# Attention heads in pairs: the values of two heads in turn, one pair late

## What is computed

```python
for l in range(2):                                  # first block
    a, g, zc, q, k, v, za, qi, ki, wi = split(h @ w_in[l])
    y_conv = silu(layer_norm(depthwise_conv31(a * sigmoid(g)))) * silu(zc)
    score  = sum_heads(relu(qi @ ki.T) * wi)        # picks the 132 keys of each query
    p      = softmax(where(chosen & causal, rope(q) @ rope(k).T / 8, -inf))   # 8 heads of 64
    y_attn = (p @ v) * silu(za)
    h      = layer_norm(alpha * h + concat(y_conv, y_attn) @ w_out[l])
# second block: 8 query heads of 64 over 2 key heads, no mask, 512 x 512
p    = softmax(axial_rope(rms(q)) @ axial_rope(rms(k)).T / 8)
y_a  = ((p @ v) * silu(gate_a)) @ w_proj_attn
g    = sigmoid(g_merge + b_merge)                   # 2 x 1024 channels
y    = g[0] * y_a + g[1] * y_b                      # y_b: a gated MLP branch
out  = rmsnorm(h + y @ w_out)
```

## Time and profile before

| | us |
|---|---|
| median of 3 runs | 1139.7 (1139.41 to 1143.92) |
| the profiled execution, its own time | 1140.32 |
| its span, first to last instruction | 1138.5 |
| TensorE busy | 1069.5 (94% of the span) |
| VectorE busy | 696.3 (61%) |
| ScalarE busy | 579.9 (51%) |
| GpSimd busy | 129.7 (11%) |
| mean granted TensorE clock | 0.972 of full |

### The profile page before, as it was taken

One profiled execution on the slowest core, in us unless ns is written; L12 is line 12 of the kernel. 1 busy time (PEld: TensorE's weight loads), 2 busy tenths in 40 slices (PEclk: granted clock), 3 DMA queues, 4 the chain that ended last, 5 costly groups with the idle time before them and its releaser, 6 DMA issues.

```text
span 1138.5 us, 16658 instructions
## 1 busy us (share of the span) xinstructions
PE 1069.5 (94%) x6484; PEld 900.7 (79%) x6484; DVE 696.3 (61%) x1553; ACT 579.9 (51%) x938; POOL 129.7 (11%) x185
## 2 busy tenths in 40 slices
PE   7998999889999899889999899969999999999997
PEld 7987898857767799789888567858888777778885
DVE  3999999965554569999989554634631332232422
ACT  6574871637333548478255643444565464554331
POOL 0000100002110100010011211223200000000001
PEclk9998999989989999999999899979999999999999
DMA  8785773735101768458546520484777525344761
GB/s 283 174 186 166 163 170 96 171 63 127 49 1 37 185 134 214 118 113 196 136 115 146 112 86 1 148 199 134 176 176 207 144 75 129 94 104 119 168 165 74
DMA packets 23822, 152.36 MB, mean 134 GB/s; under 512 B 2865, under 2 KB 3377, under 8 KB 6849
## 3 DMA queue, kind: packets, MB, share of 16 engines
q0 software_dynamic: 9648, 68.75, 32.6%
q1 hardware_dynamic: 14096, 82.55, 19.8%
HBM read 149.20 MB, written 2.10 MB: 133 GB/s over the span
## 4 chain that ended last, share of the span: by engine, by line
PE 81%; ACT 7%; DMA 5%; DVE 4%; issue 2%; POOL 0%; POOLq 0%; SPq 0%; DVEq 0%; ACTq 0%
PE psum_B L1163 19%; PE psum_A L1163 13%; PE psum_B L1196 9%; PE psum_A L1196 8%; PE psum_A L1313 6%; PE psum_B L1271 3%; DMA w_lo<-in_weights 3%; PE psum_C L1219 3%; PE psum_B L1504 3%; PE psum_B L1313 2%; PE psum_A L1517 2%; DMA w_raw<-in_weights 2%; DVE conv_acc L1600 2%; PE psum_B L1517 2%; ACT w_hi L605 2%
## 5 line engine op out<-in xcount | busy, mean ns | idle before, releaser
L1600 DVE SCALAR_TENSOR_TENSOR conv_acc<-u,vec,conv_acc 128x528 f32<-128x528 f32 (+1 forms) x240 | 172.9, 756 | 3.2
L1163 PE MATMUL psum_B<-x_hi,w_hi 128*128 128x264 f32 (+3 forms) x512 | 145.4, 323 | 8.2 <-ACT shifted L660 5.6
L1163 PE MATMUL psum_B<-x_lo,w_hi 128*128 128x264 f32 (+3 forms) x512 | 143.1, 318 | 0.0
L1163 PE MATMUL psum_B<-x_hi,w_lo 128*128 128x264 f32 (+3 forms) x512 | 142.8, 317 | 0.0
L998 POOL DMA_DIRECT2D w_lo<-in_weights x67 | 60.9, 909 | 685.8 <-ACT w_lo L606 685.8
L605 ACT ACTIVATE w_hi<-w_raw 128x2048 fp32r<-128x2048 f32 (+2 forms) x87 | 129.9, 1493 | 14.8 <-DMA w_raw<-in_weights 14.5
L606 ACT ACTIVATE w_lo<-w_raw 128x2048 fp32r<-128x2048 f32 (+2 forms) x87 | 129.3, 1486 | 0.0
L1163 PE MATMUL psum_A<-x_hi,w_hi 128*128 128x264 f32 (+2 forms) x496 | 117.9, 295 | 7.2 <-DMA w_lo<-in_weights 3.3
L1163 PE MATMUL psum_A<-x_lo,w_hi 128*128 128x264 f32 (+2 forms) x496 | 115.4, 290 | 0.0
L1163 PE MATMUL psum_A<-x_hi,w_lo 128*128 128x264 f32 (+2 forms) x496 | 115.3, 290 | 0.0
L1163 PEld LDWEIGHTS psum_B<-x_hi,w_hi 128*128 128x128 f32 (+1 forms) x512 | 89.3, 190 | 19.2 <-issue 12.5
(11 more groups left out here) (323 smaller groups left out, 2234.7 us busy)
## 6 DMA issues: line engine op xcount, KB each, us to landing
w_raw<-in_weights SPq DMA_DIRECT2D x67, 1024.0 KB, 5.7
w_lo<-in_weights POOLq DMA_DIRECT2D x65, 1024.0 KB, 8.8
x_first<-in_x_t SPq DMA_DIRECT2D x4, 528.0 KB, 7.0
h<-in_x SPq DMA_DIRECT2D x1, 2048.0 KB, 9.7
out<-h SPq DMA_DIRECT2D x4, 512.0 KB, 2.6
post_ln_g<-in_post_ln_g SPq DMA_DIRECT2D x2, 512.0 KB, 3.9
post_ln_b<-in_post_ln_b SPq DMA_DIRECT2D x2, 512.0 KB, 5.6
w_raw<-in_weights SPq DMA_DIRECT2D x2, 288.0 KB, 5.4
```

What stands on the lines that cost most here:

```text
L1163: mm = pe.matmul(ps[0:cols, i, 0:b - a], w[wp][:, kt, at:at + cols], x[xp][:, kt, a:b], start=(kt == 0 and wp + xp == 0), stop=(kt == KD - ...
L1600: got = dve.scalar_tensor_tensor(dst, src, w, dst, ALU.mult, ALU.add)
```

## The change

The attention loops of both blocks go by pairs of heads.

- `probs_times_v` and `probs_times_v2` do two heads in one call, for each key tile first the even head's matmul, then the odd head's, which write to the two halves of the partitions.
- In the first block a pair's values are computed one pair late. Turned probabilities have four buffers instead of two; the two new ones lie where the convolution's input of finished channels lay. Logits are computed four items ahead (two pairs), not two. VectorE masks and normalises the pair `i + 2` before the other work of the pair `i`; ScalarE takes the exponentials of both heads of that pair after the first copy of the pair `i`.
- In the second block both transposes of a pair come before the gate product, the values of the pair after it, and then the MLP's transpose. The weight splits woven in there go one half per pair.
- `gain` and `square_early` move to other addresses, and the load of `gain` waits for the last convolution rows of layer 1. The first output product over the last tile's convolution half moves from item 38 to 39 in layer 0.

```diff
@@ probs_times_v
-                pe.wait_ge(act_took.sem, act_took.at((l, "PT", t, hd)))
-                mm = pe.matmul(out, v[0:META, 0, hd * HD:hd * HD + HD], src[0:META, t * P:t * P + n],
-                               start=True, stop=(t == 0))
-                for j in range(1, t + 1):
-                    mm = pe.matmul(out, v[:, j, hd * HD:hd * HD + HD], src[:, (j - 1) * P:(j - 1) * P + n],
-                                   start=False, stop=(j == t))
+                pe.wait_ge(act_took.sem, act_took.at((l, "PT", t, hd + 1)))
+                for j in [0] + list(range(1, t + 1)):
+                    for odd in range(2):
+                        s, col = HD * odd, (hd + odd) * HD
+                        src = pt[i % 4 + odd]
...
+                        mm = pe.matmul(ps[s:s + HD, 0, hd // 2 * P:hd // 2 * P + n], keys, probs,
+                                       start=(j == 0), stop=(j == t))
@@ TensorE, first block
+                attention_logits(l, 0)
+                attention_logits(l, 2)
+                for i in range(0, n, 2):
                     turn_probs(l, i)
                     if i:
-                        probs_times_v(l, i - 1)
-                probs_times_v(l, n - 1)
+                        probs_times_v(l, i - 2)
+                    woven(i)
+                    turn_probs(l, i + 1)
+                    if i + 4 < n:
+                        attention_logits(l, i + 4)
+                    woven(i + 1)
+                probs_times_v(l, n - 2)
@@ ScalarE, first block
+                exps(l, 0)
+                exps(l, 1)
+                for i in range(0, n, 2):
+                    take_probs_t(l, i)
+                    if i + 2 < n:
+                        exps(l, i + 2)
+                        exps(l, i + 3)
+                    woven(i)
+                    take_probs_t(l, i + 1)
+                    woven(i + 1)
@@ VectorE, first block
+                for i in range(0, n, 2):
+                    if i + 2 < n:
+                        masked_logits(l, i + 2)
+                        masked_logits(l, i + 3)
+                        normalise(l, i + 2)
+                        normalise(l, i + 3)
+                    for op in middle[i] + middle[i + 1]:
+                        y_part(l, *op[1:])
+                    woven(i)
+                    woven(i + 1)
@@ TensorE, second block
+            merge_gate(0)
+            for i in range(0, n, 2):
+                turn_probs2(i)
+                turn_probs2(i + 1)
+                if i:
                     merge_gate(i // 2)
-                if i % 2 and i < 8:
+                if i + 4 < n:
+                    logits2(i + 4)
+                    logits2(i + 5)
+                probs_times_v2(i)
+                if i < 8:
                     turn_mlp(i // 2)
```

More of the change, by code:

```diff
@@ L832, in _, with woven @@
                 n = len(items[l])
[L833 to L837, removed]
+                def woven(i):
                     for op in todo[i]:
@@ L1408, in _, with woven @@
                     pe.wait_ge(rope_made.sem, rope_made.at((l, "k", c)))
-                attention_logits(l, 0)
-                for i in range(n):
-                    if i % 2 == 0 and i + 2 < n:
-                        attention_logits(l, i + 2)
+                def woven(i):
                     for op in todo[i]:
@@ L1846, in _, with woven @@
                 n = len(items[l])
-                masked_logits(l, 0)
-                masked_logits(l, 1)
-                for i in range(n):
-                    normalise(l, i)
-                    for op in middle[i]:
-                        y_part(l, *op[1:])
-                    if i + 2 < n:
-                        masked_logits(l, i + 2)
+                def woven(i):
                     for op in todo[i]:
@@ L1871, in _ @@
                             y_part(l, *op[1:])
+                masked_logits(l, 0)
+                masked_logits(l, 1)
+                normalise(l, 0)
+                normalise(l, 1)
+                for i in range(0, n, 2):
+                    if i + 2 < n:
+                        masked_logits(l, i + 2)
[6 more added lines that the diff above has]
+                    woven(i + 1)
                 y_part(l, "attn", 4)
@@ L2089, in _ @@
             n = len(items2)
-            max2(0)
-            max2(1)
-            for i in range(n):
-                normalise2(i)
-                if i > 1 and i % HEADS == 1:
-                    attn2_part(i // HEADS - 1)
-                if i + 2 < n:
-                    max2(i + 2)
-                if i % 2 and i < 8:
+            for i in range(4):
+                max2(i)
+            normalise2(0)
+            normalise2(1)
+            for i in range(0, n, 2):
+                if i + 2 < n:
+                    normalise2(i + 2)
+                    normalise2(i + 3)
+                if i and i % HEADS == 0:
+                    attn2_part(i // HEADS - 1)
+                    attn2_lo(i // HEADS - 1)
+                if i + 4 < n:
+                    max2(i + 4)
+                    max2(i + 5)
+                if i < 8:
                     mlp_low(i // 2)
-                if i > 2 and i % HEADS == 2:
-                    attn2_lo(i // HEADS - 1)
             attn2_part(3)
```

75 lines of the change are left out of this document (38 added, 37 removed).

## The result

The changed kernel takes 1113.3 us (median of 4 runs, 1111.81 to 1114.4) against 1139.56; the ratio is 0.976, with a 95% interval of 0.9734 to 0.9786. It is faster, and inside the range given (1088 to 1129), but 15 us above the 1098 forecast. The range is 41 us wide and holds two of the three rivals too (1113 and 1128), so that being inside it decides nothing between them; the trace has to. The profiled execution took 1111.81, its span is 1110.0.

A forecast was written before the change was run, and what follows sets the result against it. TensorE, busy 1069.5 of 1138.5 us, was taken as the bound, with VectorE nearer from 197 to 249. Gains 15.5 + 3.6 + 15.4 + 4 + 8 - 2 - 2 = 42.5 off 1140.3 gave 1098 us, range 1088 to 1129.

The forecast's parts named there:

- Halves overlap: Value matmuls: two heads on different column halves take one head's time, 16 passes in 1.02 us; chance .72, forecast 1098.
- Layer 0 from 249: First block, layer 0, from 249 us: 15.4 us saved on 14 pairs' values, plus 4 us of waits recovered.
- the dip at 331 us: Layer 0, 331.6 to 341 us: granted clock .69 behind the longest wait for probabilities, 2.9 us lost.
- my 6.8: Layer 0: 3.9 us of TensorE waits for probabilities plus 2.9 us lost to low clock; 4 counted as gain.
- a whole pair more of cover: Layer 0's waits for probabilities: four items between logits and transposes instead of two; 4 of 6.8 us taken.
- Tap stages and the middle of layer 1: First block, 197 to 249 us and layer 1's middle: net loss of 2 us, ends +2 and -8.
- The .5 us per pair: Tap stages: VectorE idles about .5 us per pair between masking and normalising, while ScalarE does its exponential.
- Layer 1 from 652.5: First block, layer 1, from 652.5 us: cheaper values in 7 pairs give 9.0 us, of which 8 taken.
- Ends: Ends of both layers: later first output product delays weight loads and lengthens the w_lo wait; -2 us, from 0 to -5.
- No overlap: Rival: the column halves don't run side by side, only steps and waits are saved, 11.9 us, 1128; chance .16.
- Slower through exposed loads: Rival: weight loads of value passes come out of hiding, .14 us in each of 592 passes, 1211; chance .05.
- Eaten by other engines: Rival: halves overlap, but tap stages, layer ends, unrecovered waits and ScalarE's copies leave 27.5 us gained, 1113; chance .07.

The follow-up runs named there:

- the other pair of traces: Traces of two kernels: the kernel before with only the second block's part of the change, 1122.75 us; with only the first block's part, 1129.97 us.
- second block only: The kernel before with only the second block's part of the change, first block unchanged: 1122.75 us, ratio 0.9854.
- the kernel with work between: The changed kernel, with VectorE in the first block doing the even item's other work between masking and normalising a pair: 1095.21 us, ratio 0.9621.
- one head after the other: The changed kernel with the value loops swapped, so the two heads' value matmuls no longer run in turn: 1137.07 us, ratio 0.9976.

## Why the prediction came out as it did

**Halves overlap: right, and decisive.** Pairs of value passes start 7 ns apart and the next pair .11 later, 8.52 a pair against 8.50 forecast. The MLP's pairs take 9.84 against 9.93, with a wait of .63 for `mlp_lo` where I left .8; two gate products of the changed kernel's TensorE timeline:

```profile
904.67 0.47 PE L1176 MATMUL psum_B<-x_hi,w_hi 128*128 128x512 f32 x1 [0.63 <-DVE mlp_lo L2049]
...
914.51 0.47 PE L1176 MATMUL psum_B<-x_hi,w_hi 128*128 128x512 f32 x1 [0.63 <-DVE mlp_lo L2049]
```

The block gave 17.5 against 19.1; its first pair alone waits 1.67 for `mlp_lo`, which I had not looked at.

**Layer 0 from 249: mis-sized, and here is two thirds of the miss.** 15.4 + 4 was forecast, 9.9 came (a shift from +1.5 to -8.5; 6.1 by the other pair of traces). The values were priced rightly: the eight pairs of tiles 3 and 4 gave 15.7: their 10.2 of values, and the old waits and the dip at 331 us, which are gone. The dip itself was partly luck of the trace I read: second block only has the same code and the same waits there (3.9, 3 times), and its granted clock stays full,

```profile
331.00:341.00 10.00, 10.00 (x57) 7.59 (x57) 4.84 (x9) 3.45 (x9) 1.91 (x3) 1.00 0.01 2
```

so that these pairs gave 12.6 in that pair of traces. Of my 6.8, the 2.9 belonged to one execution.

The step that failed is the sentence that these waits have a whole pair more of cover. The logits have it. The first transpose of a pair has less than before: between it and the transpose ahead of it, whose copy must be out of the bank, stood a head's values, the logits and the coming item's other work, and now in items 17 and 21 only the logits; and the copy stands in ScalarE's queue behind two exponentials and a split. New waits of 7.1, and two stretches of low clock behind them (4 x .32 + 7 x .40 = 4.1), make 11.2, which is about the 5.7 us lost there and the 5.2 that the pairs of tiles 1 and 2 should have given (the rest of the 15.4), 10.9. I wrote that ScalarE is busy 51.5 of 119 and so not near; from 249 to 290 it is busy 26.2 of 41, and what it is busy with stands ahead of the copy.

**Tap stages and the middle of layer 1: the sign right, the mechanism wrong.** -2 was forecast; 1.5 lost until 250 and 2.7 from 562 to 652 make -4.2. The .5 us per pair took ScalarE as free when VectorE asks. Its exponentials stand behind a copy that waits for TensorE. VectorE's idle time ahead of reciprocals between 632 and 715 is

```profile
DVE prob_rsums L1730 <- ACT exps L729: 27.3, 8, 9.0
```

and over both layers' attention, 197 to 720, 61.9 us in 35 pieces, against 19.0 in 19 in the kernel before; .5 in each of 14 pairs would have been 7. Compared with before this cost little, since the old order lost as much elsewhere (with it, the kernel is 18 us slower still). The forecast left out that 18 us lay there for the taking.

**Layer 1 from 652.5:** 8 forecast, 6.0 came. **Ends:** -2 forecast; -2.6 behind layer 0 and +1.8 behind layer 1, and by the second pair of traces .6 is lost behind layer 0 and 1.1 won behind layer 1, so the two ends together can't be told from nothing. That the later first product costs something isn't shown, nor that it doesn't. The wait for `w_lo` behind layer 0 is 2.8, not longer than the 2.99 of the earlier trace rows. The stretch behind layer 0 has 3.4 us more lost to the lower clock than before; whether the shorter attention ahead of it causes that, no run here tells.

**The rivals.** No overlap (1128): out, by the starts. Slower through exposed loads (1211): out, the loads of 136 ns stay hidden with 16 passes in 1.03. By the rule of the Trainium skill that the prediction cites ("TensorE: Matmul & The Clock Gate", "Part 3: Packing small matmuls — row/col tiling"), read by row groups alone, they would have shown; the trace does not agree with that reading. Eaten by other engines (1113): its number fits to a microsecond, 15 better than my own, and much of its story too, for ScalarE's copies did come last; but at another place (the next transposes and not the values), with little at the layers' ends and the old waits won back.

In sum 42.5 was forecast and 28.5 of span came (26.3 by the medians); of the 14 missing, 9.5 are in layer 0, 2.2 in the tap stages and the middle, 2.0 in layer 1, 1.6 in the second block, and the ends gave 1.2 back.

## What to carry to other kernels

Two matmuls of 64 output columns on different halves of the array, issued in turn, cost the time of one; look for such pairs wherever a head is 64 wide. When an order is changed on one engine, draw for each queue what stands between an operation and the hand over that it waits for: busy shares near 50% hid a chain in which VectorE waited for ScalarE, ScalarE for TensorE, and TensorE was in a product. Put independent work between an engine's two steps that have another engine's step between them, and try it even where the change in front of you seems to have gained what it should. When two traces are compared, compare the length of the same work and not when it starts, and find out first how much it differs between two executions of the same code.

## What the runs showed that I had not expected

With one head after the other the second block's 16 passes take 1.51 and not 1.90: in the middle of the run two passes start within some 50 ns of each other, as if the second head's first ones ran beside the first head's last. In the first block, where each head begins with the 16 meta keys, there is no such thing (2.32 for tile 3). What decides this wasn't tried.

Fewer waits can bring back more than their own length. In layer 1 the kernel with work between runs at 1.00 where the changed one has 0.95 over 133 us: 6.7 us less of waiting came with 6.4 us less of busy time for the same matmuls. It is not a fixed price: in layer 0 the same 3.9 us of waits went with a clock of .69 for 9.4 us in one trace and with the full clock in the other.
